# Norm 1 and the first modulations in the set-up and in the tail of the expert block, in a two-layer hybrid trunk on one Trainium2 core

## The reference

```python
def trunk_layer(x, cond, lb, cached, ...):
    mod = jax.nn.silu(cond) @ mod_w + mod_b
    sh1, sc1, g1, sh2, sc2, g2 = jnp.split(mod[:, None, :], 6, axis=-1)
    h = rms_norm(x, norm1_g) * (1.0 + sc1) + sh1
    qa, ia, fza, fzb, ga, qg, kg, vg, qw, kw, vw = split_proj(h @ w_in)
    ...
    x = x + g1 * (jnp.concatenate([o_a, o_g, o_w], axis=-1) @ w_out)
    h = rms_norm(x, norm2_g) * (1.0 + sc2) + sh2
    x = x + g2 * moe(h, router_w, router_b, w_gate_up, w_down)
    return x, new
```

## Time and profile before

| | |
|---|---|
| timed runs | 1710.44, 1718.92, 1719.37 us (median 1718.92) |
| the profiled execution, own time | 1705.26 us |
| its span | 1703.5 us |
| PE busy, mean granted clock | 1397.6 us (82%), 0.907 of full |
| DVE, ACT, POOL busy | 629.2, 362.7, 200.1 us |
| DMA moved | 263.43 MB |

### The profile page before, as it was taken

How to read it: one execution, slowest core, us unless ns; L and a number is a source line. 1 busy time by engine, 2 the same in 40 slices (tenths; PEclk the granted TensorE clock), 3 DMA queues, 4 the chain that set the end, 5 groups by cost and what they waited for, 6 DMA issues and landing times. The chain is left out here.

```text
span 1703.5 us, 22336 instructions
## 1 busy us (share of the span) xinstructions
PE 1397.6 (82%) x8151; PEld 829.7 (49%) x8152; DVE 629.2 (37%) x1372; ACT 362.7 (21%) x840; POOL 200.1 (12%) x151
## 2 busy tenths in 40 slices
PE   2699999889996579999039999997899963999950
PEld 2466555666553534444035655565665552444420
DVE  1226465454443501111411454735454434111115
ACT  2310011333333111111122100123333240111113
POOL 0104420100000010000210244101000000000010
PEclk9799999899998589999569999997999975999985
DMA  8311011593002379996390111108600045899933
GB/s 301 106 53 53 1 55 39 193 316 162 1 1 93 133 258 368 366 364 236 137 306 1 53 53 50 42 3 296 189 2 1 1 143 185 279 375 368 358 114 133
DMA packets 118798, 263.43 MB, mean 155 GB/s; under 512 B 10264, under 2 KB 27312, under 8 KB 118576
## 3 DMA queue, kind: packets, MB, share of 16 engines
q1 hardware_dynamic: 105744, 214.97, 36.2%
q0 software_dynamic: 8064, 29.36, 4.5%
q10 hardware_dynamic: 4896, 17.83, 2.6%
HBM read 230.88 MB, written 42.27 MB: 160 GB/s over the span
## 5 line engine op out<-in xcount | busy, mean ns | idle before, releaser
L652 PE MATMUL PS<-W,hT 128*128 128x512 f32 (+1 forms) x640 | 274.1, 555 | 0.0
L1700 PE MATMUL PS<-W,T 128*128 128x512 f32 x544 | 242.4, 599 | 4.5 <-ACT T L1742 4.5
L1700 PEld LDWEIGHTS PS<-W,T 128*128 128x128 f32 x544 | 104.3, 192 | 135.7 <-issue 129.9
L652 PEld LDWEIGHTS PS<-W,hT 128*128 128x128 f32 x640 | 109.9, 189 | 74.5 <-issue 60.3
L1718 PE MATMUL PS<-W,T 128*128 128x512 f32 x272 | 126.0, 607 | 1.4 <-ACT T L1766 1.4
L824 DVE COPY_PREDICATED W<-levelmask,PS 128x512 f32<-128x512 uint8 (+2 forms) x96 | 77.6, 809 | 104.1 <-PE PS L593 103.9
L1143 PE MATMUL PS<-W,hT 128*128 128x512 f32 x240 | 115.0, 607 | 0.0
L1788 DVE TENSOR_TENSOR T<-PS,T 128x256 f32<-128x256 f32 x34 | 14.5, 426 | 240.3 <-ACT T L1753 240.3
L1091 PE MATMUL PS<-cst,T 128*128 128x128 f32 x432 | 77.2, 300 | 30.4 <-ACT T L1209 22.3
L556 PE MATMUL PS<-hT,W 128*128 128x512 f32 x192 | 98.4, 594 | 2.8 <-DVE hT L795 2.8
L593 PEld LDWEIGHTS PS<-W 64*128 64x128 f32 x1120 | 69.0, 187 | 56.0 <-issue 38.9
(11 more groups left out here) (249 smaller groups left out, 1814.9 us busy)
## 6 DMA issues: line engine op xcount, KB each, us to landing
W<-in_w_gate_up SPq DMA_DIRECT2D x34, 2048.0 KB, 13.0
W<-in_mod_w SPq DMA_DIRECT2D x24, 2048.0 KB, 14.2
W<-in_w_down SPq DMA_DIRECT2D x34, 1024.0 KB, 10.7
y_rows<-T ACTq DMA_DIRECT2D x34, 512.0 KB, 9.2
y_rows<-cst SPq DMA_DIRECT2D x2, 7680.0 KB
W<-in_w_in SPq DMA_DIRECT2D x10, 1024.0 KB, 11.3
W<-in_w_in SPq DMA_DIRECT2D x4, 2048.0 KB, 7.9
T<-mod_rows SPq DMA_DIRECT2D x16, 512.0 KB, 6.1
```

The costliest lines, as they stand in the source:

```text
L652: last = pe.matmul(PS[:, u % 4, 0:512 - at], hT[:, k, col(t)], ring[:, slot, k, at:512], start=(k == 0), stop=(k == KC - 1))
L1700: last = pe.matmul(PS[:, 2 + par, :], hgT[:, par, k, :], w[:, k, :], start=(k == 0), stop=(k == KC - 1))
```

## The change

- The set-up block of layer 0 now also loads the first four pieces of `mod_w` and the groups "qf" and "bv", computes the modulations and norm 1, and writes `hT`. In place of scaling a tile and turning it with the identity, PE multiplies the tile by a diagonal matrix `diag` that holds the tile's factors of 1/rms.
- The scan block starts with the loads of the caches and goes to the gates. The filler rows are issued there.
- In layer 0 the attention block issues three pieces of layer 1's `mod_w` at its end, the norm 2 block the fourth. The norm 2 block multiplies them and prepares shift and scale (in both layers; in layer 1 the loads are skipped and the products are not used).
- The expert block's SP list issues "qf" and "bv" of layer 1 after the last expert tile's weights. Its combine also takes squares (ACT), powers (POOL, tile by tile), diagonals (ACT), products with the diagonal (PE) and writes `hT` (DVE, ACT). The gate multiplication of tile 3 moves to POOL. In layer 1 the combine is followed by the multiplication with the final gains and the stores; the final block is gone.
- The semaphores are cleared by one instruction for the whole range.

```diff
             def _(sp):
-                sp.dma_start(cst[:, :], consts).then_inc(s_ld, 16)
-                sp.dma_start(mask_f32, masks).then_inc(s_ld, 16)
-                sp.dma_start(crow[:, 0, :], c_ctx.rearrange("(a b) -> a b", b=P)).then_inc(s_ld, 16)
...
-                sp.dma_start(x[:, 1:NT, :], x_sample[0].rearrange("(t p) n -> p t n", p=P)).then_inc(s_ld, 16)
-                sp.dma_start(rbias[:, :], router_b.partition_broadcast(P)).then_inc(s_ld, 16)
-                sp.wait_ge(s_ld, 8 * 16)
...
+                sp.dma_start(cst[:, :], consts).then_inc(s_c, 16)
+                sp.dma_start(crow[:, 0, :], c_ctx.rearrange("(a b) -> a b", b=P)).then_inc(s_c, 16)
+                sp.dma_start(crow[:, 1, :], c.rearrange("o (a b) -> (o a) b", b=P)).then_inc(s_c, 16)
+                sp.dma_start(crow[:, 2, :], hgrn_lb.rearrange("d l (f b) -> (d l f) b", b=P)).then_inc(s_c, 16)
+                for n in range(MOD1):
+                    if n == 0:
+                        sp.dma_start(x[:, 0, :], x_prompt[0]).then_inc(s_x[0], 16)
+                    if n < 2:
+                        sp.dma_start(x[:, 2 * n + 1:2 * n + 3, :], x_sample[0, 2 * n * P:(2 * n + 2) * P, :]
+                                     .rearrange("(t p) n -> p t n", p=P)).then_inc(s_x[n], 16)
+                    sp.dma_start(pmodw[n], mod_w[0, :, col(n, MODW)].rearrange("(k p) n -> p k n", p=P)).then_inc(s_pw[n], 16)
+                    if n == 0:
+                        sp.wait_ge(s_nz, 1)
+                        load_mod_rows(sp, mod_b[0, 0:MOD1 * MODW], MOD1, modrow, s_nrow)
+                        load_mod_rows(sp, norm1_g[0], 2, gain1, s_nrow)
+                load_ring("qf")
+                sp.dma_start(mask_f32, masks).then_inc(s_mk, 16)
+                sp.dma_start(rbias[:, :], router_b.partition_broadcast(P)).then_inc(s_mk, 16)
+                sp.wait_ge(s_nmr, MOD1)
+                load_ring("bv")
+                sp.wait_ge(s_ngl, 5 * 16)
...
+                for t in range(NT):
+                    pool.wait_ge(s_nsq, t + 1)
+                    pool.tensor_scalar(nms[:, t:t + 1], nms[:, t:t + 1], EPS, None, ALU.add).then_inc(s_neps, 1)
+                    pool.wait_ge(s_neps, t + 1)
+                    pool.tensor_tensor(nrs[:, t:t + 1], nms[:, t:t + 1], minus_half[:, 0:1], ALU.pow).then_inc(s_nrs, 1)
...
+                def turn_tile(t):
+                    pe.wait_ge(s_ndg, t + 1)
+                    if t >= 3:
+                        pe.wait_ge(s_nev, t - 2)
+                        pe.wait_ge(s_nea, t - 2)
+                    for k in range(KC):
+                        last = pe.matmul(PS[:, next_bank(t, 3) + k // 4, col(k % 4)], x[:, t, col(k)], diag[:, t % 2, :],
+                                         start=True, stop=True)
+                    last.then_inc(s_ntr, 1)
...
+                for n in range(MOD1):
+                    mod(n)
+                    if n < 3:
+                        turn_tile(n)
+                pe.wait_ge(s_nch, 2)
+                for n in range(MOD1):
+                    last = pe.transpose(PS[:, 6, col(n)], modrow[:, n, :], ident)
+                last.then_inc(s_nmt, 1)
+                for t in range(3, NT):
+                    turn_tile(t)
...
+                for t in range(NT):
+                    mean(t)
+                    if t < 3:
+                        diagonal(t)
+                act.wait_ge(s_nch, 3)
+                for t in range(NT):
+                    act.wait_ge(s_ntr, t + 1)
+                    cond = 1 if t else 0
+                    for k in range(4, KC):
+                        last = act.activation(hT[:, k, col(t)], PS[:, next_bank(t, 3) + 1, col(k % 4)], ACT.Identity,
+                                              bias=shift1[:, k, cond:cond + 1], scale=scale1[:, k, cond:cond + 1])
+                    last.then_inc(s_nea, 1)
+                    if t + 3 < NT:
+                        diagonal(t + 3)
...
+                dve.wait_ge(s_nrow, 4 * 16)
+                dve.wait_ge(s_nmr, MOD1)
+                rows = modrow.rearrange("p s n -> p (s n)")
+                dve.tensor_tensor(rows, PS[:, 7, :], rows, ALU.add).then_inc(s_nch, 1)
+                dve.wait_ge(s_nch, 1)
+                scales = modrow[:, 2:4, :]
+                dve.scalar_tensor_tensor(scales, scales, 1.0, gain1, ALU.add, ALU.mult).then_inc(s_nch, 1)
...
+                dve.wait_ge(s_nch, 3)
+                for t in range(NT):
+                    dve.wait_ge(s_ntr, t + 1)
+                    cond = 1 if t else 0
+                    for k in range(4):
+                        last = dve.tensor_scalar(hT[:, k, col(t)], PS[:, next_bank(t, 3), col(k)],
+                                                 scale1[:, k, cond:cond + 1], shift1[:, k, cond:cond + 1],
+                                                 ALU.mult, ALU.add)
+                    last.then_inc(s_nev, 1)
+                dve.wait_ge(s_mk, 2 * 16)
+                dve.tensor_copy(levelmask[:, :, :, :].rearrange("p a b c -> p (a b c)"), mask_f32)
...
-                    for n in range(3):
-                        load_mod(sp, n)
...
                     sp.dma_start(ck[:, 0, :], cgk[0, layer].rearrange("s h d -> s (h d)")).then_inc(s_cl, 16)
...
+                    for n in range(3):
+                        load_next_mod(sp, n)
...
+                    for n in range(3):
+                        next_mod(n)
                     pe.wait_ge(s_rw, 2 * 16)
...
+                    next_mod(3)
...
                     last.then_inc(s_slt, 1)
+
+                    pe.wait_ge(s_nch, 2)
+                    for n in range(MOD1):
+                        last = pe.transpose(PS[:, 4, col(n)], modrow[:, n, :], ident)
+                    last.then_inc(s_nmt, 1)
...
+            POOL_GATED = [3]
...
                     load_down(sp, load_last(sp), 0, 2)
+                    for name in ("qf", "bv"):
+                        slot, pieces = GROUPS[name]
...
+                            sp.dma_start(ring[:, slot, :, at:at + n], w_in[1, :, o:o + n].rearrange("(k p) n -> p k n", p=P),
+                                         cond=(layer < 1)).then_inc(s_ngl, 16)
...
+                        if t in POOL_GATED:
+                            pool.wait_ge(s_cm, combined["pair", t])
+                            ya = yab[:, t, 0, :]
+                            pool.tensor_tensor(ya, ya, g2b[:, 1 if t else 0, :], ALU.mult).then_inc(s_cp, 1)
+                        if t >= 1:
+                            rstd(t - 1)
+                    rstd(NT - 1)
...
+                    def mean(t):
+
+                        act.wait_ge(s_cm, combined["residual", t])
+                        act.activation(yab[:, t, 1, :], x[:, t, :], ACT.Square, scale=1.0 / 32,
+                                       accum_out=nms[:, t:t + 1]).then_inc(s_nsq, 1)
...
+                    act.wait_ge(s_nch, 3)
+                    weigh(0)
+                    weigh(1)
+                    for t in range(NT):
+                        mean(t)
+                        if t + 2 < NT:
+                            weigh(t + 2)
+                        if t >= 1:
+                            with act.If(layer < 1):
+                                diagonal(t - 1)
+                                if t >= 2:
+                                    next_evac(t - 2)
+                    with act.If(layer < 1):
+                        diagonal(NT - 1)
+                        next_evac(NT - 2)
+                        next_evac(NT - 1)
...
+                    for t in range(NT):
+                        add_pair(t)
+                        if t >= 1:
+                            add_residual(t - 1)
+                    add_residual(NT - 1)
+                    with dve.If(layer < 1):
+                        for t in range(NT):
+                            next_evac(t)
...
-                    for s in layer_sems:
-                        pool.sem_clear(s)
+                    pool.sem_clear(range(layer_sems[0].num, layer_sems[-1].num + 1))
```

445 lines of the change are left out of this document (226 added, 219 removed).

## The result

The changed kernel takes 1668.74 us (median of 4 runs, 1667.23 to 1670.11) against 1719.14 for the kernel before, timed beside it (4 runs, 1710.44 to 1720.74). The ratio is 0.9717, 95% interval 0.9682 to 0.9751: faster by 50.4 us, where the prediction had 46.8 and 1672.

A forecast was written before the change was run, and what follows sets the result against it. PE was busy for 82% of the span, but the change touches stretches where it has little to do, the start being set by loads, then norm 1. Terms -7.8 + 2.0 - 33.6 - 7.4 = -46.8 us gave 1672, range 1656 to 1688.

The forecast's parts named there:

- signs of being wrong: DVE not idling in the combine, gates over 15 us after the jump, or a block in between changing by over 3 us.
- Set-up, -7.8: Start of layer 0: without the loading hole, block ends near 50 us, gates run as if started at 57.6 instead of 65.38.
- Next modulations, +2.0 for two layers: Norm 2 block: PE's extra products cost nothing in its idle time; the turn of four rows adds 1.0 a layer.
- The wheel: Combine: ACT and DVE wait for each other each tile, 6.2 us a turn instead of 3.72; last addition 8.35 us later.
- The rival that it does not turn: Combine: ACT and DVE keep to 3.72 us a tile, giving 2 x 8.35 us more gain: 1655; chance 0.08.
- The gate of tile 3, "hidden": Combine: POOL's gate multiplication takes 2.3 us, unseen because DVE needs it only 6 us after it can start.
- Clears, 8.7 each: End of each layer: 9.3 us from first clear to jump shrinks to 0.6 for one clear and the barrier.
- Jump to gates, 9.4: Loop turn into layer 1: after the first load, 9.4 us including landing and turns, then 1.5 for the clock.
- the rival in which it stays at half: Gates: PE's clock stays at 1.2 GHz throughout, two stretches add 100 us, time 1772; chance 0.03.
- Loads behind the last expert's, nothing: End of layer 0's experts: 4.2 MB more loads, 12 us, cost nothing; 12 if they met the gathers in full.
- Branches: Rival: skipped branches cost, up to 3.4 us in each layer on DVE behind the last addition, time 1679; chance 0.10.
- End of the program, -7.4: After layer 1's combine: last addition at 1684.9, then multiplications, clear and barrier, ending at 1696.1 instead of 1703.5.

The follow-up runs named there:

- kernel with one clear: Kernel before with one edit: the 132 single semaphore clears at the loop's turn become one clear of the whole range; 1694.88 us against 1715.96, ratio 0.9875.
- The late products: Changed kernel with one edit: PE's three products in norm 2 wait for all five tiles' square means, so run directly ahead of the first turn; 1649.59 us, ratio 0.9641.
- the kernel with both sets of products: Changed kernel with one addition: norm 2's three early products stay, and three are made again directly ahead of the first turn; 1664.90 us, ratio 0.9694.

## Why the prediction was right

It was right in sum and in direction, but not in every term. On the profiled pair the change is 37.9 and not 46.8; that the median still came within 3.3 us is partly luck with the execution of before that was profiled. Of the signs of being wrong that the prediction names, one came true: a block in between was to change by no more than 3 us, and norm 2 of layer 0 grew by 8.1, while the attention block of layer 1 got 3.5 shorter (220.0 us instead of 223.5, at a mean granted clock of 0.977 instead of 0.954 with the same work). Point by point:

- **Set-up, -7.8.** The gates start 9.8 earlier and the attention block, past the slower first gates, 8.4 earlier. Right. The forecast block end near 50 was 50.2. From gates to attention pass 1.4 more, and 1.5 was forecast for the pause; but the kernel with one clear, in which the turns stand right ahead of the gates, also needs 1.4 more there, so that the pause does it is not shown.
- **Next modulations, +2.0 for two layers.** Here a step failed. "PE has three products more ahead of its first turn [...] it was idle for 13.57 us before that turn. [...] Both at nothing." No engine waits for those products, and the fourth is hidden too. But with them at the block's start the turns and logits of layer 0 ran at 0.50 throughout, 6.0 us more, and the rows landed later, 1.6 and 2.0 us more in the two layers; with 0.4 each behind the logits, the turn of four rows among them (forecast 1.0), and -0.2 from turns to logits in layer 1, that makes +8.1 and +2.2. I costed the work, and neither what it does to the clock of the work behind it nor what it does to the loads beside it. The late products show what the clock is worth, 18.5 us.
- **The wheel.** Right in mechanism and size: a turn takes 5.94, forecast 6.2; idle 2.25, forecast 2.4; ACT's order alone is worth 6.9 and 7.2 us a layer, while the forecast had 8.35 for the whole delay and 9.25 was measured from the first sum on. The rival that it does not turn is out.
- **The gate of tile 3, "hidden".** Wrong: it held DVE's addition for 2.04 us, which makes the move a loss of 0.8 a layer. Without it the delay from the first sum on would have been 7.2, an estimate (9.25 - 2.04). The step took POOL's 2.3 us as free, as DVE needs their result only 6 us later; it did not ask what DVE does in between. The rule of the Trainium skill ("SBUF — State Buffer", section "SBUF: two separate sides"), which the prediction gave beside the sum, was right, with up to 2.3 a layer; 2.04 was measured.
- **Clears, 8.7 each.** Measured 8.08 and 7.81 with nothing else changed. The one clear and the barrier take 1.4 together (856.1 to 857.5) and not 0.6.
- **Jump to gates, 9.4.** From 857.5, where the block ends, to 866.06 pass 8.6. The clock's loss was larger than thought: gates to attention took 253.2 us in layer 1 against 250.7, so 2.6 and not 1.5, of which again 1.6 came in the kernel with one clear without a pause. The granted clock was at 1.00 within 6 us of the first gate in both layers, so the rival in which it stays at half is out.
- **Loads behind the last expert's, nothing.** Right: ACT's wait for the gathers is about 6.9 us as before, and undoing the move makes no difference there but makes the scan block 7.4 longer.
- **Branches.** Nothing that can be seen in either layer. In layer 1, where DVE skips the writes of `hT`, its next operation starts at 1653.66, without a gap behind the last addition. In layer 0, where it skips the final multiplications, its branch takes 0.06 us, beside its own last writes. That rival is out.
- **End of the program, -7.4.** From the last addition to the end pass 11.9 us, forecast 11.2. Right; the end moved less than summed only since the addition was late.

So of the 8.9 us missing on the profiled pair, norm 2 holds 8.3 (10.3 measured, 2.0 forecast), the two combines 1.8 (2 x 9.25 against 16.7) and the experts ahead of them 3.7, which lies within the spread of that stretch. The start, the attention blocks and the way to the gates of layer 1 gave some 5 back. The range and the chance for faster rested on the clears, the loads and norm 1, which are large and came out as summed.

## What to carry to other kernels

Work put into an engine's idle time can look free, because nobody waits for it. On TensorE ask also at which clock the next work will run: with the same three products at the block's start the two norm 2 blocks took 10 us more than before, and with them directly ahead of the turns 8 us less. When two engines feed each other tile by tile, count how many tiles ahead each list runs; one tile more of lead took 14 us off. And look at plain housekeeping on the path: 132 single clears stood there for 16 us.

## What the runs showed of the hardware

- A semaphore clear over the whole range takes 0.74 us (the kernel before with one clear) to 0.83 (the changed kernel); one semaphore takes 0.037, and 132 in a row, with their issue, about 8 us more than the range.
- Small GpSimd operations pay too beside VectorE's operations of two inputs: the addition of one column took 0.22 us alone and 1.20 beside them, the power 0.57 and 1.46.

```profile
1652.61 1.20 POOL L1775 TENSOR_SCALAR small<-small 128x1 f32<-128x1 f32 x1 [3.80 <-ACT W L1899]
...
1653.90 1.46 POOL L1777 TENSOR_TENSOR small<-small,minus_half 128x1 f32<-128x1 f32 x1
```

- The granted clock fell from 1.00 to 0.50 within matmuls that followed each other without a gap (at about 550 us in the kernel with both sets of products). Work without gaps did not by itself hold it.
- The kernel before spreads more than the changed one: spans of 1702.5 to 1720.8 with mean clocks from 0.907 down to 0.895, against 1664.8 to 1673.2 and 0.919 to 0.912. Its other executions were not profiled, so where it loses those 18 us is open, and with it where the 12 us between the medians' gain and the traces' gain lie. The trace of the same kernel with one clear shows only that its gates can start at 0.50, for 1.4 and 1.6 us.
